# First attention mixer: scores in two PSUM banks by turns, turned rows in one bank instead of two

## The chip, the cores and the metric

The kernel runs on one core of one Trainium2 chip. The metric is the device time of one launch in microseconds (us), the median of several runs; lower is better. TensorE is PE in the profile, VectorE DVE, ScalarE ACT, GpSimd POOL and SyncE SP.

## What is computed

A trunk of two layers over 512 tokens of width 1024. Each layer is half a SwiGLU block, an attention mixer and another half SwiGLU block; each sub-layer has an RMS norm, a shift and scale made from a condition vector, and a gated residual add. The first layer's mixer ("mixA", layer "A" in the code) is the one that is changed. Cut to what matters:

```python
def moba_mixer(h, w_qkv, w_o, cos, sin):
    qkv = (h @ w_qkv).reshape(B, S, 3, N_HEADS, HEAD_DIM)
    q, k = apply_rope(qkv[:, :, 0], cos, sin), apply_rope(qkv[:, :, 1], cos, sin)
    return moba_attention(q, k, qkv[:, :, 2]).reshape(B, S, ATTN_DIM) @ w_o
# moba_attention: 2 blocks of 256 tokens, top 3 of the past blocks: with 512 tokens
# every past block is chosen, so it is causal softmax attention, 16 heads of 64
p = softmax(where(causal, q @ k.T * scale, -inf)); o = p @ v
```

## The kernel before, in words

All matrix products run in float32 split into a high and a low part, three passes each (L412, L413, L414: high by high, low by high, high by low). Weights come by DMA in units of 512 KB into w_raw (L397); ScalarE copies the high part into w_hi (L403), VectorE, sometimes GpSimd, subtracts to get w_lo (L407).

**The mixer's work in steps.** mixA handles 16 heads in four groups of four. A head has four steps, one for each 128 query tokens, so there are 64 steps, numbered here 0 to 63; step n has n % 4 + 1 tiles of 128 keys. The steps of one group run beside the q, k and v projections of the next group ("substeps" on TensorE), and the last group's beside the output projection. The order of work on each engine is written out by hand as program code; engines meet through counting semaphores. For step n the chain is:

- TensorE: *score n*, two matmuls (L805, L806) into a PSUM bank.
- VectorE: *negmax n*, which scales and masks the scores, writes them to SBUF and keeps the row maximum (L2157, with its read-accumulator row behind it).
- ScalarE: exp n (L1965); VectorE: reciprocal of the sum, n (L2177); GpSimd: scaling by it (L2358).
- TensorE: *turn n*, n % 4 + 1 transposes of the probabilities into a PSUM bank (L839). The bank holds the "turned rows".
- ScalarE: *copy n*, the high part of the turned rows (L1989); VectorE: *subtraction n*, the low part (L2221). Both read the bank of the turned rows. After four steps TensorE multiplies by v (L849), and ScalarE and VectorE fold the result (L1998, L2233).

**Where they stand.** The programs are skewed. TensorE's `begin(n)` does score n, one or two substeps of the projection (L412 to L414) where the table has any for that step, and then turn n-2. VectorE's `begin(n)` does negmax n, reciprocal n-1, the fold of a head where one is due, and then subtraction n-3; behind it stand, by hand-written tables, other work of the step: a w_lo subtraction (L407), half of a rotary multiply (L1528), the low part of rotated rows (L1577). ScalarE's `begin(n)` does exp n, then what its tables say (w_hi, L403; high part of rotated rows, L1572; v, L1607), and at the end copy n-2.

**The banks.** PSUM has eight banks. In mixA the projections take 0 to 3, the scores have bank 4, the heads' output 5, and the turned rows take 6 and 7 by turns. So score n waits until negmax n-1 has read bank 4, and turn n waits until subtraction n-2 has read its bank. The second mixer, layer "B", has scores in 4 and 3 and turned rows in 6 and 7; it keeps both.

Of the kernel before, what the change touches and what calls it, by code (L numbers as in the profile page):

```python
# [32 lines left out]
P = 128  # L33
# [146 lines left out]
def build(nc, x_t, c_col, ada_first, ada, ada_bias, gains, gate_up, down, mixa_w, kv_w, mixb_w, cos_t, sin_t,  # L180
          mask_a, mask_b, lanes_in, ident_in, out):
    with ExitStack() as ctx:  # L182
# [3 lines left out]
        def sb(stack, name, shape, dt=F32):  # L186
            return stack.enter_context(nc.sbuf_tensor(name, shape, dt))
# [10 lines left out]
        ident = sb(ctx, "ident", [P, P])  # L198
# [31 lines left out]
        with ExitStack() as mixer_space:  # L230
# [10 lines left out]
            pt_hi = sb(mixer_space, "pt_hi", [P, 4, 4, P], F32R)  # L241
# [17 lines left out]
        ps = ctx.enter_context(nc.psum_tensor("ps", [P, 8, 512], F32))  # L259
# [12 lines left out]


        def scores(layer, st):
            return ps[:, 4 if layer == "A" or st % 2 == 0 else 3, :]

        def turned(st):
            return ps[:, 6 + st % 2, :].rearrange("p (n q) -> p n q", n=4)

        o_ps = ps[:, 5, :]  # L280

# [4 lines left out]
        def second_pt(tile):  # L286
            return flat(tile)[:, 2 * S:6 * S].rearrange("p (n i q) -> p n i q", n=4, i=4)

        pt_a = ((pt_hi[:], pt_lo[:]), (second_pt(q_st), second_pt(k_hi)))
        spare_slots = v_out[:].rearrange("p j t a d -> p (j t a d)")[:, 0:2 * S].rearrange("p (n s) -> p n s", n=2)  # L290

        def p_slot(layer, st):
            n = st % SLOTS[layer]
            return probs[:, n, :] if n < 6 else spare_slots[:, n - 6, :].bitcast(F32)
# [47 lines left out]
        def per_mixer(name):  # L342
            return {"A": sem(name + "_a"), "B": sem(name + "_b")}

        s_done, negmax_done, exp_done = per_mixer("s_done"), per_mixer("negmax_done"), per_mixer("exp_done")
        factor_done, scaled_done = per_mixer("factor_done"), per_mixer("scaled_done")
        t_done, pt_hi_done, pt_lo_done = per_mixer("t_done"), per_mixer("pt_hi_done"), per_mixer("pt_lo_done")
# [396 lines left out]
        def pe_mixer(pe, name):  # L744
            layer = name[-1]
            is_a = layer == "A"
# [46 lines left out]
            def score(st):  # L793
                h, i, sl = st // 4, st % 4, st // 4 % 2
                if i == 0:
                    pe.wait_ge(k_landed[h % 2], 32 * ((hd0 + h) // 2 + 1))
                    pe.wait_ge(q_landed[h % 2], 16 * ((hd0 + h) // 2 + 1))
                    if h % 4 == 0 and not is_a:
                        pe.wait_ge(q_direct, h // 4 * 16 + 32)
                tile, s_ps = slice(i * P, (i + 1) * P), scores(layer, st)  # L800
                if is_a:
                    if st >= 1:
                        pe.wait_ge(negmax_done["A"], st)
                    past = slice(0, (i + 1) * P)
                    nc.tensor.matmul(s_ps[:, past], q_st[:, 0, sl, tile], k_hi[:, 0, sl, past], start=True, stop=False)  # L805
                    nc.tensor.matmul(s_ps[:, past], q_st[:, 0, sl, tile], k_lo[:, 0, sl, past],  # L806
                                     start=False, stop=True).then_inc(s_done["A"], 1)
                    return


                if st >= 2:
                    pe.wait_ge(negmax_done["B"], 2 * st - 2)
                if st >= 6 and i == 2:
                    pe.wait_ge(exchanged, 2 * h - 1)
                q, past = q_st[:, sl, 0, tile], slice(max(i - 1, 0) * P, (i + 1) * P)
                kh, kl = k_hi[:, sl, 0, past], k_lo[:, sl, 0, past]
                o = s_ps[:, P if i == 0 else 0:2 * P]
                nc.tensor.matmul(o, q, kh, start=True, stop=False)
                nc.tensor.matmul(o, q, kl, start=False, stop=True)
                for b in (1, 2):  # L820
                    o, q = s_ps[:, (1 + b) * P:(2 + b) * P], q_st[:, sl, b, tile]
                    nc.tensor.matmul(o, q, k_hi[:, sl, b, tile], start=True, stop=False)
                    mm = nc.tensor.matmul(o, q, k_lo[:, sl, b, tile], start=False, stop=True)
                mm.then_inc(s_done["B"], 1)
# [7 lines left out]

            def transpose_p(st):
                pe.wait_ge(scaled_done[layer], st + 1)
                if st >= 2:
                    pe.wait_ge(pt_lo_done[layer], st - 1)
                i = st % 4
                for n in range(i + 1) if is_a else range(1 if i == 0 else 0, 4):
                    mm = nc.tensor.transpose(turned(st)[:, n, :], p_slot(layer, st)[:, n * P:(n + 1) * P], ident[:])  # L839
                mm.then_inc(t_done[layer], 1)  # L840

            def weigh_a(h):
# [44 lines left out]
            def begin(st, first=(), second=()):  # L887
                if st < ROWS:
                    score(st)
                for part in first:  # L890
                    part()
                back = st - lag
                if is_a and back >= 5 and back % 4 == 1:
                    weigh_a(back // 4 - 1)
                if not is_a and back >= 4 and back % 4 < 2:
                    weigh_b(back // 4 - 1, back % 4)
                for part in second:
                    part()
                if 0 <= back < ROWS:
                    transpose_p(back)  # L900
                if not is_a and st % 4 == 0 and 4 <= st <= ROWS:
                    exchange(st // 4 - 1)
# [1036 lines left out]
        def act_mixer(act, name):  # L1939
            layer = name[-1]  # L1940
            is_a, lag = layer == "A", LAG[layer]
# [36 lines left out]
            def round_pt(st):  # L1978
                i = st % 4
                act.wait_ge(t_done[layer], st + 1)  # L1980
                if is_a:
                    h = st // 4
                    if h >= 2 and i == 0:
                        act.wait_ge(pv_done["A"], h - 1)
                    src, dst = turned(st)[:, 0:i + 1, :], pt_a[h % 2][0][:, 0:i + 1, i, :]
                else:
                    first = 1 if i == 0 else 0
                    src, dst = turned(st)[:, first:4, :], pt_hi[:, i, first:4, :]
                nc.scalar.copy(dst, src).then_inc(pt_hi_done[layer], 1)  # L1989

            def fold_copy(h):
# [14 lines left out]
            def collect(st):  # L2006
                if (st - lag) % 4 == 1 and st - lag >= 5:
                    fold_copy((st - lag) // 4 - 1)
                if 0 <= st - lag < ROWS:
                    round_pt(st - lag)  # L2010
# [137 lines left out]
        def dve_mixer(dve, name, g_block, col_n, stored):  # L2148
            layer = name[-1]
            is_a, lag = layer == "A", LAG[layer]  # L2150
# [4 lines left out]
            def masked(st, cols, mask, lowest):  # L2155
                dve.sem_inc(carrier, 1)
                nc.vector.tensor_tensor_reduce(  # L2157
                    out=p_slot(layer, st)[:, cols], in0=scores(layer, st)[:, cols], in1=mask, scale=-(HD ** -0.5),
                    scalar=FAR, op0=ALU.add, op1=ALU.min, accum_out=lowest).then_inc(negmax_done[layer], 1)
# [54 lines left out]
            def split_pt(st):  # L2214
                i = st % 4
                dve.wait_ge(pt_hi_done[layer], st + 1)
                first = 1 if i == 0 and not is_a else 0
                src = turned(st)[:, 0:i + 1, :] if is_a else turned(st)[:, first:4, :]
                hi, lo = (pt[:, 0:i + 1, i, :] if is_a else pt[:, i, first:4, :]
                          for pt in (pt_a[st // 4 % 2] if is_a else (pt_hi, pt_lo)))  # L2220
                nc.vector.tensor_tensor(lo, src, hi.bitcast(F32), ALU.subtract).then_inc(pt_lo_done[layer], 1)  # L2221
# [29 lines left out]
            def collect(st):  # L2251
                if (st - lag) % 4 == 1 and st - lag >= 5:
                    fold_add((st - lag) // 4 - 1)
                if 0 <= st - lag < ROWS:
                    split_pt(st - lag)
# [458 lines left out]
```

## Time and profile before

| what | value |
|---|---|
| median of 3 runs | 2371.2 us (2370.36 to 2376.19) |
| profiled execution: its time, its span from first to last instruction | 2373.33 us, 2371.5 us |
| granted TensorE clock, mean | 0.994 of full |
| TensorE busy / VectorE / ScalarE / GpSimd, share of span | 99% / 55% / 37% / 12% |
| attention steps of mixA in the trace | 457 to 646 us |

The profile comes from one execution with a hardware profiler. Its busy time of TensorE counts overlapping matmuls: a matmul of 512 columns is shown 0.39 us long while the next starts 0.23 us after it. So a short stop of TensorE can lie inside "busy", and the start times of successive rows say more than the busy share.

### The profile page before, as it was taken

How to read it: one execution, taken by the hardware profiler on the slowest of the kernel's cores; microseconds unless marked ns; L12 is line 12 of the kernel's file. 1: busy time of each engine (PE TensorE's matmuls, PEld its weight loads, DVE VectorE, ACT ScalarE, POOL GpSimd, SP SyncE). 2: the span in 40 equal slices, each digit the busy share in tenths (PEclk: the TensorE clock that was granted, in tenths of full speed). 3: DMA queues.
4: the chain of work that ended last, by engine and by line, in shares of the span. 5: the costliest groups of instructions: out<-in, count | busy, mean ns of one | idle time of the engine just before them, and what ended most of it. 6: DMA issues, size and time to landing. Idle time of an engine off the chain costs nothing. (4 is left out here: it accounts for less than half of the span.)

```text
span 2371.5 us, 31348 instructions
## 1 busy us (share of the span) xinstructions
PE 2337.0 (99%) x11240; PEld 1941.8 (82%) x11245; DVE 1315.5 (55%) x2084; ACT 876.4 (37%) x1397; POOL 288.8 (12%) x373
## 2 busy tenths in 40 slices
PE   9999999999999999999999999999999999999998
PEld 6888888788878888888888888888888887888886
DVE  7555544776675554465554555544777766333333
ACT  3322223456543332233332333322456654333221
POOL 0000000244300000003232000000134531000000
PEclk9999999999999999999999999999999989999999
DMA  6666543577456564338777666543788862333332
GB/s 249 198 188 192 177 133 100 200 245 247 159 157 197 184 187 131 115 97 273 238 236 252 233 196 189 159 144 96 229 294 295 297 237 73 97 97 97 93 97 85
DMA packets 128896, 424.90 MB, mean 179 GB/s; under 512 B 14112, under 2 KB 22944, under 8 KB 128288
## 3 DMA queue, kind: packets, MB, share of 16 engines
q1 hardware_dynamic: 111392, 356.55, 46.9%
q0 software_dynamic: 17408, 67.12, 8.1%
q8 instruction: 54, 0.88, 0.2%
q14 instruction: 42, 0.34, 0.0%
HBM read 352.84 MB, written 69.21 MB: 178 GB/s over the span
## 5 line engine op out<-in xcount | busy, mean ns | idle before, releaser
L407 DVE TENSOR_TENSOR w_lo<-w_raw,w_hi 128x1024 fp32r<-128x1024 f32 (+2 forms) x382 | 467.8, 1225 | 610.2 <-ACT w_hi L403 609.8
L412 PE MATMUL ps<-h_hi,w_hi 128*128 128x512 f32 x1872 | 741.7, 396 | 9.2 <-POOL h_lo L2101 2.5
L414 PE MATMUL ps<-h_hi,w_lo 128*128 128x512 f32 x1872 | 730.9, 390 | 0.0
L413 PE MATMUL ps<-h_lo,w_hi 128*128 128x512 f32 x1872 | 730.6, 390 | 0.0
L403 ACT CAST w_hi<-w_raw 128x1024 fp32r<-128x1024 f32 (+2 forms) x388 | 395.6, 1020 | 752.5 <-PE ps L414 735.6
L412 PEld LDWEIGHTS ps<-h_hi,w_hi 128*128 128x128 f32 x1872 | 352.8, 188 | 84.6 <-issue 6.1
L414 PEld LDWEIGHTS ps<-h_hi,w_lo 128*128 128x128 f32 x1872 | 352.4, 188 | 74.9
L413 PEld LDWEIGHTS ps<-h_lo,w_hi 128*128 128x128 f32 x1872 | 353.0, 189 | 68.7 <-issue 0.2
L412 PE MATMUL ps<-act_hi,w_hi 128*128 128x512 f32 x704 | 275.3, 391 | 0.0
L414 PE MATMUL ps<-act_hi,w_lo 128*128 128x512 f32 x704 | 274.1, 389 | 0.0
L413 PE MATMUL ps<-act_lo,w_hi 128*128 128x512 f32 x704 | 273.9, 389 | 0.0
L1553 POOL TENSOR_TENSOR rotated<-tmp 128x512 f32<-128x512 f32 x32 | 44.5, 1391 | 1309.7 <-DVE tmp L1107 1229.7
L1420 DVE TENSOR_TENSOR prod<-ps,silu_g 128x512 f32<-128x512 f32 x86 | 59.5, 692 | 260.1 <-ACT silu_g L1376 260.1
L976 DVE SCALAR_TENSOR_TENSOR ada_acc<-ada_raw,c_act,ada_acc 128x1024 f32<-128x1024 f32 x126 | 161.2, 1280 | 0.7
L412 PEld LDWEIGHTS ps<-act_hi,w_hi 128*128 128x128 f32 x704 | 132.1, 188 | 31.0 <-issue 3.9
L414 PEld LDWEIGHTS ps<-act_hi,w_lo 128*128 128x128 f32 x704 | 132.2, 188 | 27.6
L413 PEld LDWEIGHTS ps<-act_lo,w_hi 128*128 128x128 f32 x704 | 132.2, 188 | 27.2
L1376 ACT ACTIVATE silu_g<-ps 128x512 f32<-128x512 f32 x86 | 51.5, 599 | 252.1 <-PE ps L414 251.7
L1376 ACT ACT_TABLE_LOAD x30 | 38.5, 1283 | 135.0 <-PE ps L414 135.0
L412 PE MATMUL ps<-w_hi,kv_h_hi 128*128 128x512 f32 x192 | 74.8, 390 | 0.0
L413 PE MATMUL ps<-w_lo,kv_h_hi 128*128 128x512 f32 x192 | 74.7, 389 | 0.0
L414 PE MATMUL ps<-w_hi,kv_h_lo 128*128 128x512 f32 x192 | 74.7, 389 | 0.0
(206 smaller groups left out, 2798.3 us busy)
## 6 DMA issues: line engine op xcount, KB each, us to landing
w_raw<-gate_up SPq DMA_DIRECT2D x176, 512.0 KB, 3.7
ada_raw<-ada SPq DMA_DIRECT2D x144, 512.0 KB, 4.6
w_raw<-down SPq DMA_DIRECT2D x80, 512.0 KB, 3.6
w_raw<-kv_w SPq DMA_DIRECT2D x48, 512.0 KB, 3.8
w_raw<-mixa_w SPq DMA_DIRECT2D x34, 512.0 KB, 4.2
w_raw<-mixb_w SPq DMA_DIRECT2D x34, 512.0 KB, 4.9
kb<-rot_st POOLq DMA_DIRECT2D x24, 512.0 KB, 4.9
kb<-att POOLq DMA_DIRECT2D x24, 512.0 KB, 5.2
```

Of the source, the lines that this page charges most:

```text
L403: nc.scalar.copy(w_hi[:, slot, 0:n], w_raw[:, slot, 0:n]).then_inc(w_hi_done, 1)
L407: eng.tensor_tensor(w_lo[:, slot, 0:n], w_raw[:, slot, 0:n], w_hi[:, slot, 0:n].bitcast(F32), ALU.subtract).then_inc(w_lo_done[slot], 2)
L412: nc.tensor.matmul(out_ap, l_hi, r_hi, start=start, stop=False, skip_group_check=skip)
L413: nc.tensor.matmul(out_ap, l_hi, r_lo, start=False, stop=False, skip_group_check=skip)
L414: return nc.tensor.matmul(out_ap, l_lo, r_hi, start=False, stop=stop, skip_group_check=skip)
L976: nc.vector.scalar_tensor_tensor(out=ada_acc[:], in0=ada_raw[:, slot, :], scalar=c_act[:, k:k + 1], in1=ada_acc[:], op0=ALU.mult, op1=ALU. ...
L1376: nc.scalar.activation(silu_g[:, b, :], ps[:, 2 * b, :], ACT.Silu).then_inc(silu_done, 1)
L1420: nc.vector.tensor_tensor(prod[:, b, :], ps[:, 2 * b + 1, :], silu_g[:, b, :], ALU.mult).then_inc(pair_free, 1)
L1553: nc.gpsimd.tensor_tensor(*operands(0), ALU.subtract).then_inc(rope_done, 1)
```

## The change

In layer "A" the scores get bank 4 on even steps and bank 6 on odd ones, and all turned rows go to bank 7. Score n then waits for negmax n-2 instead of n-1, and turn n for subtraction n-1 instead of n-2. Nothing else differs: no instruction is added, removed or moved on any engine, and layer "B" is as it was.

```diff
         def scores(layer, st):
-            return ps[:, 4 if layer == "A" or st % 2 == 0 else 3, :]
-
-        def turned(st):
-            return ps[:, 6 + st % 2, :].rearrange("p (n q) -> p n q", n=4)
+            return ps[:, 4 if st % 2 == 0 else 6 if layer == "A" else 3, :]
+
+        def turned(layer, st):
+            return ps[:, 7 if layer == "A" else 6 + st % 2, :].rearrange("p (n q) -> p n q", n=4)
...
                 if is_a:
-                    if st >= 1:
-                        pe.wait_ge(negmax_done["A"], st)
+                    if st >= 2:
+                        pe.wait_ge(negmax_done["A"], st - 1)
...
             def transpose_p(st):
                 pe.wait_ge(scaled_done[layer], st + 1)
-                if st >= 2:
-                    pe.wait_ge(pt_lo_done[layer], st - 1)
+                if st >= (1 if is_a else 2):
+                    pe.wait_ge(pt_lo_done[layer], st if is_a else st - 1)
```

(The other lines of the diff pass the layer to `turned` where ScalarE and VectorE read the bank.)

TensorE's program at the start of the attention steps, score 1: k_hi, k_lo and q_st are the operands of a score.

```order
 L413 MATMUL ps<-h_lo,w_hi 128x512
 L414 MATMUL ps<-h_hi,w_lo 128x512
-L805 MATMUL ps<-k_hi,q_st 128x256 [waits negmax_done_a]
+L805 MATMUL ps<-k_hi,q_st 128x256
 L806 MATMUL ps<-k_lo,q_st 128x256
 L412 MATMUL ps<-h_hi,w_hi 128x512
```

Score 1 no longer waits; the scores after it keep a wait, for a count that is one lower.

TensorE's program two steps on (its begin(3)), turn 1: probs are the probabilities, and pt_lo_done_a counts the subtractions.

```order
 L413 MATMUL ps<-h_lo,w_hi 128x512
 L414 MATMUL ps<-h_hi,w_lo 128x512
-L839 MATMUL ps<-ident,probs 128x128 [waits scaled_done_a]
+L839 MATMUL ps<-ident,probs 128x128 [waits pt_lo_done_a,scaled_done_a]
 L839 MATMUL ps<-ident,probs 128x128
 L805 MATMUL ps<-k_hi,q_st 128x128 [waits negmax_done_a,q_landed1,k_landed1]
```

Turn 1 now waits for subtraction 0; the turns after it waited for a subtraction before and now wait for the next one. No row has moved on TensorE, and the other engines' programs are the same row for row.

## Rows read from the trace of the kernel before

**Rows 1.** Waits of TensorE, 450 to 660 us: total, times, longest

```profile
PE ps L805 <- DVE negmax L2157: 3.2, 4, 1.2
PE ps L839 <- DVE pt_lo L2221: 1.0, 1, 1.0
PE ps L805 <- issue: 0.9, 1, 0.9
PE ps L412 <- DVE x L2117: 0.9, 1, 0.9
PE ps L412 <- POOL h_lo L2101: 0.5, 1, 0.5
```

**Rows 2.** Timeline of TensorE: start, length, row, idle before; score 1, turn 28, score 31

```profile
460.27 0.39 PE L805 MATMUL ps<-k_hi,q_st 128*128 128x256 f32 x1 [1.19 <-DVE negmax L2157]
...
541.71 0.27 PE L839 MATMUL ps<-ident,probs 128*128 128x128 f32 x1
542.67 0.50 PE L805 MATMUL ps<-k_hi,q_st 128*128 128x512 f32 x1 [0.69 <-DVE negmax L2157]
```

**Rows 3.** Timeline, SyncE's load of q for score 4, and score 4

```profile
463.43 0.43 SPq L1755 DMA_DIRECT2D q_st<-qa  x1
...
469.67 0.30 PE L805 MATMUL ps<-k_hi,q_st 128*128 128x128 f32 x1 [0.86 <-issue]
```

**Rows 4.** Timeline of TensorE, second group of heads: turns 18, 24 and 26

```profile
520.25 0.49 PE L839 MATMUL ps<-ident,probs 128*128 128x128 f32 x3
...
533.77 0.27 PE L839 MATMUL ps<-ident,probs 128*128 128x128 f32 x1
...
538.91 0.49 PE L839 MATMUL ps<-ident,probs 128*128 128x128 f32 x3
```

**Rows 5.** Timeline of VectorE, second group: subtractions 17, 23, 25 and 27

```profile
520.27 0.43 DVE L2221 TENSOR_TENSOR pt_lo<-ps,pt_hi 128x256 fp32r<-128x256 f32 x1
...
534.32 0.69 DVE L2221 TENSOR_TENSOR k_hi<-ps,q_st 128x512 fp32r<-128x512 f32 x1 [1.00 <-ACT q_st L1989]
...
539.19 0.42 DVE L2221 TENSOR_TENSOR pt_lo<-ps,pt_hi 128x256 fp32r<-128x256 f32 x1
...
542.73 0.69 DVE L2221 TENSOR_TENSOR pt_lo<-ps,pt_hi 128x512 fp32r<-128x512 f32 x1
```

**Rows 6.** Timeline of ScalarE: work ahead of copies 23 and 27, and the copies

```profile
532.76 1.05 ACT L1572 CAST rot_st<-rotated 128x1024 fp32r<-128x1024 f32 x1
533.71 0.58 ACT L1989 CAST q_st<-ps 128x512 fp32r<-128x512 f32 x1
...
541.17 1.05 ACT L403 CAST w_hi<-w_raw 128x1024 fp32r<-128x1024 f32 x1 [0.28 <-PE ps L414]
542.12 0.58 ACT L1989 CAST pt_hi<-ps 128x512 fp32r<-128x512 f32 x1
```

**Rows 7.** Timeline, third group: turn 44 (TensorE) and subtraction 43 (VectorE)

```profile
590.82 0.30 PE L839 MATMUL ps<-ident,probs 128*128 128x128 f32 x1
...
592.54 0.69 DVE L2221 TENSOR_TENSOR pt_lo<-ps,pt_hi 128x512 fp32r<-128x512 f32 x1 [0.74 <-ACT pt_hi L1989]
```

**Rows 8.** Timeline, last group: turns 50 and 51, subtractions 49 and 50

```profile
609.91 0.55 PE L839 MATMUL ps<-ident,probs 128*128 128x128 f32 x3
...
611.30 0.42 DVE L2221 TENSOR_TENSOR pt_lo<-ps,pt_hi 128x256 fp32r<-128x256 f32 x1
...
611.88 0.63 PE L839 MATMUL ps<-ident,probs 128*128 128x128 f32 x4 [0.99 <-DVE pt_lo L2221]
...
612.84 0.56 DVE L2221 TENSOR_TENSOR pt_lo<-ps,pt_hi 128x384 fp32r<-128x384 f32 x1 [0.70 <-ACT pt_hi L1989]
```

**Rows 9.** Busy time by windows (us; engines; PEclk; DMA share, GB/s): mixA, and mixB's end

```profile
457.00:646.00 189.00, 182.47 (x1085) 159.61 (x1084) 126.59 (x338) 111.15 (x251) 79.69 (x104) 1.00 0.67 230
...
1895.00:1905.00 10.00, 6.43 (x42) 5.80 (x42) 7.05 (x25) 5.13 (x16) 3.76 (x8) 0.93 0.92 332
1905.00:1915.00 10.00, 10.00 (x47) 9.56 (x47) 4.42 (x15) 4.29 (x14) 2.78 (x5) 0.56 0.92 325
```

More of the change, by code:

```diff
@@ L834, in transpose_p @@
                 pe.wait_ge(scaled_done[layer], st + 1)
-                if st >= 2:
-                    pe.wait_ge(pt_lo_done[layer], st - 1)
+                if st >= (1 if is_a else 2):
+                    pe.wait_ge(pt_lo_done[layer], st if is_a else st - 1)
                 i = st % 4
                 for n in range(i + 1) if is_a else range(1 if i == 0 else 0, 4):
-                    mm = nc.tensor.transpose(turned(st)[:, n, :], p_slot(layer, st)[:, n * P:(n + 1) * P], ident[:])
+                    mm = nc.tensor.transpose(turned(layer, st)[:, n, :], p_slot(layer, st)[:, n * P:(n + 1) * P], ident[:])
                 mm.then_inc(t_done[layer], 1)
@@ L1984, in round_pt @@
                         act.wait_ge(pv_done["A"], h - 1)
-                    src, dst = turned(st)[:, 0:i + 1, :], pt_a[h % 2][0][:, 0:i + 1, i, :]
+                    src, dst = turned(layer, st)[:, 0:i + 1, :], pt_a[h % 2][0][:, 0:i + 1, i, :]
                 else:
                     first = 1 if i == 0 else 0
-                    src, dst = turned(st)[:, first:4, :], pt_hi[:, i, first:4, :]
+                    src, dst = turned(layer, st)[:, first:4, :], pt_hi[:, i, first:4, :]
                 nc.scalar.copy(dst, src).then_inc(pt_hi_done[layer], 1)
@@ L2217, in split_pt @@
                 first = 1 if i == 0 and not is_a else 0
-                src = turned(st)[:, 0:i + 1, :] if is_a else turned(st)[:, first:4, :]
+                src = turned(layer, st)[:, 0:i + 1, :] if is_a else turned(layer, st)[:, first:4, :]
                 hi, lo = (pt[:, 0:i + 1, i, :] if is_a else pt[:, i, first:4, :]
```

## The prediction

> **What bounds the kernel now.** TensorE is busy for 99% of the span. In mixA I read the waits of TensorE first. Five kinds are all there are, 6.5 us together: scores that wait for negmax (3.2 us, four times), a turn that waits for a subtraction (1.0 us), one "issue" wait (0.9 us) and two waits of the output projection (0.9 and 0.5 us) [rows 1]. All else that TensorE does there it does back to back, so a delay that is put on it is made up nowhere unless it falls into one of these waits. The reader should see next that the old score wait costs little and where: score 1 stands idle for 1.19 us, and score 31 starts 0.96 us after turn 28 although only one small transpose lies between [rows 2]. Scores 15 and 47 are the same place in the other groups; these are the steps that have no projection work between two scores.
>
> Then I read, for each step n, where turn n starts and where subtraction n-1 ends. The change makes the first wait for the second. Before the change this distance is free, so it may be negative, and in 34 of 63 steps it is negative or too short. That is what the prediction rests on.
>
> **The wait that is removed.** Scores 15, 31 and 47 each come up by 0.96 us less the 0.06 us that a 128-column transpose takes (a quarter of the 0.23 us from one 512-column matmul to the next): 0.9 us, 2.7 us for three. Score 1 comes up by 1.19 us idle and 0.16 us that the row of the matmul before it hides (0.39 us shown, next start after 0.23 us): 1.35 us. But score 4 follows in the same stretch and waits 0.86 us for "issue", which is the landing of its q and k: the q load left at 463.43 and the score began at 469.67 [rows 3]. The load hangs on weights' split and on stores, not on score 1, so an earlier score 1 only makes score 4 wait longer. I take 0 for score 1; if the load does come earlier, it is a gain of 1.35 us.
>
> **The wait that is added.** Queued behind a waiting turn n on TensorE are score n+3, the next projection matmuls and so everything. What a waiting TensorE needs after the end of the instruction that it waits for is seen twice: turn 51 began at 611.88, 0.16 us after subtraction 49 ended (611.30 + 0.42) [rows 8]. With 0 and 0.16 us as its bounds I take 0.10 us; 0.05 us more or less is 1 us over some twenty waits. The shortfall of turn n is then end of subtraction n-1, plus 0.10, less start of turn n.
>
> Second group, steps 16 to 31 [rows 4, 5]:
> - turn 18: 520.27 + 0.43 + 0.10 - 520.25 = 0.55 us.
> - turn 24: 534.32 + 0.69 + 0.10 - 533.77 = 1.34 us.
> - turn 26: 539.19 + 0.42 + 0.10 - 538.91 = 0.80 us.
> - turn 28: 542.73 + 0.69 + 0.10 - 541.71 [rows 2] = 1.81 us.
> - turns 20 and 22 come out between the first and the third of these in the same two views, 0.39 and 0.86 us.
>
> Turns 18 to 26 are four small ones and turn 24 one large, with turn 28 six in all, 5.75 us. Two more, turns 21 and 25, are short by under 0.4 us but drop out: VectorE was then working off a queue and does not shift with TensorE's new delay. For the same reason I take 0.4 off turn 22 and 0.3 off turn 26. That leaves 5.05 us.
>
> Why don't the later ones vanish once TensorE has waited? Because the two large ones have a cause that moves with TensorE. Copy 23 runs at 533.71 behind rotated rows' high part (532.76, 1.05 us), and copy 27 at 542.12 behind w_hi, which started at 541.17 when TensorE released it (0.28 us idle, ended by PE) [rows 6]. A TensorE that is later releases them later. VectorE's subtraction follows the copy at once (534.32 with 1.00 us of idle ended by ACT, [rows 5]).
>
> Groups: the second gives 5.05 - 0.9 = **+4.1 us**. The first repeats it without turn 18 (no fold is due there yet): 4.5 - 0.9 = **+3.6 us**. The third also has the output's inputs on ScalarE, which puts copies back: turn 44 is short by 592.54 + 0.69 + 0.10 - 590.82 = 2.51 us [rows 7] in place of 1.81; turn 40 by 1.0 instead of 1.3; turns 34, 36, 38 and 42 by 0.55, 0.39, 0.47 and 0.4. Turn 46 too is short, by 0.9 us, but the matmul right behind its score waited 0.9 us for VectorE's addition to x anyway [rows 1], so this costs nothing. Sum 5.3 - 0.9 = **+4.4 us**.
>
> Last group: three steps stand without projection work there. Turn 50 is short by 611.30 + 0.42 + 0.10 - 609.91 = 1.91 us. Turn 51 by 612.84 + 0.56 + 0.10 - 611.88 = 1.62 us, but it already waited 0.99 us, and both its old wait and subtraction 50 move with turn 50, so only 0.1 us is new. Turns 48, 49 are short by 0.5 us together, turns 52 to 60 by about 1.6 us. The 0.5 us wait for h_lo behind it [rows 1] and a little of VectorE's queue are filled by the delay, 0.75 us off. **+3.4 us**.
>
> Sum: 3.6 + 4.1 + 4.4 + 3.4 = **15.5 us**. After mixA nothing gives it back: what follows is a serial norm and TensorE-bound GEMM. The profiled execution took 2373.33 us, span 2371.5; it would become 2388.8. It stood 2.1 us above the median of the runs, 2371.2, so I give 2371.2 + 15.5 = **2386.7 us**.
>
> **A page against the trace.** The bank that is given up matters because in each step both ScalarE and VectorE read what TensorE wrote, one after the other: copy 23 from 533.71 to 534.29, subtraction 23 from 534.32 to 535.01 [rows 5, 6], so with one bank the next turn can't overlap either. The Trainium skill, "PSUM — Partial Sum Buffer", section "PSUM bank collisions raise a hardware error", says that TensorE, ScalarE and VectorE may not touch the same bank and partitions at once, and asks for semaphores by bank; by that rule the new wait can be neither dropped nor narrowed to columns, and the score's second bank is paid for in full. A sum by the old score wait alone would be -4.1 us; by the new one it is +15.5. The trace agrees as far as it goes: copy and subtraction of a step never overlap in these rows.
>
> **The rivals.**
> - *Each wait resets the lag.* While TensorE waits, VectorE and ScalarE catch up, and the shortfalls behind it in the group vanish; only the largest of each group is left: 1.34 or 1.81, less 0.9, in two groups, 2.5 - 0.9 in the third, 1.9 in the last. 0.9 + 0.9 + 1.6 + 1.9 = 5.3 us, 2376.5 us, within 0.3%. For it: VectorE has 35% of idle in mixA (126.59 of 189 us busy [rows 9]). Against: turns 24 and 28 hang on work that TensorE itself releases. Chance 0.12.
> - *The other side: the turns were never late.* The subtraction has room before the turn if VectorE and ScalarE, now given score 1, 15, 31, 47 earlier, pull ahead for the rest of the group. Place: turns 20 to 28; price: all shortfalls gone, gain 2.7 + 1.35 = 4.1 us, 2367.1 us. It decides for a gain if less than 4.1 us of the 18.2 us of shortfalls that I counted (15.5 + 2.7) survives. Against it: the earlier scores number four, and each comes at a group's end, behind the turns in question. Chance 0.04.
> - *No absorption.* All 34 shortfalls, read as above but with 0.07 us in place of 0.10, come to 26.1 us (5.5, 6.0, 8.8 and 5.9 by group), less 2.7: +23.4, 2394.6 us. Chance 0.08.
> - *The clock falls.* In all of mixA the granted clock is 1.00, that is 2.4 GHz, with TensorE busy 182.47 of 189 us. At mixB's end TensorE was busy 6.43 of 10 us, and in the next 10 us the clock was 0.56, so nearly all of it at 1.2 GHz [rows 9]: 0.44 x 10 = 4.4 us of work lost. The last group of mixA now gets 3.5 us of waits within 6 us (turns 50 and 51). 15.5 + 4.4 = 19.9, 2391.1 us. Chance 0.10. The Trainium skill, "TensorE: Matmul & The Clock Gate", part 1, says that the throttled clock is the default and only activity lifts it; by that rule such a gap of waits may cost a stretch at half rate, and the trace at mixB's end agrees.
>
> The forecast itself keeps 0.66.
>
> **How the numbers follow.** 0.3% is 7.1 us, about what a measurement of this kernel can tell from no change. The forecast's own range: lower end, only the turns whose cause moves with TensorE and turn 50, 3.15 - 0.9 twice, 3.5 - 0.9, 1.9, less 1.35 for score 1: 7.7 us, 2378.9; upper end the 23.4 us above, 2394.6. The range reaches down into the first rival and to the upper bound: 2376 to 2394.5. Slower than by 0.3%: 0.66, 0.08 and 0.10, 0.84. Within 0.3%: the first two rivals, 0.12 and 0.04, less 0.02 for a gain above 7.1 us, which none of the cases reaches and which I keep as what I have not seen: 0.14 and 0.02.
>
> **What the changed profile would show.** Waits of TensorE in mixA: the negmax rows at L805 gone or nearly, and L839 waiting for pt_lo (L2221) some 20 times for 12 to 19 us in place of 1.0. Score 4 begins at about the same time as before. Turns 24 and 28 are late by more than a microsecond each against the row before them, and the four groups lengthen by 3 to 5 us each. ScalarE, VectorE and GpSimd keep their busy time; the second mixer keeps its length. I am wrong if L839's waits are few, or if they are many but other waits disappear by as much, or if work outside mixA changes.

## The result: 19 us slower

The changed kernel takes 2391.9 us (median of 4 runs, 2391.0 to 2392.8) against 2372.6 us of the kernel before in the same comparison: a ratio of 1.0081, 95% interval [1.0069, 1.0093]. A second measurement gave 1.0083 [1.0069, 1.0096]. The forecast was 2386.7 us, range 2376 to 2394.5, slower with a chance of 0.84.

The waits of TensorE in the profile after, 450 to 690 us, answer to [rows 1]. Columns: who waited for whom, us in total, times, longest.

```profile
PE ps L839 <- DVE pt_lo L2221: 11.9, 15, 2.2
PE ps L839 <- DVE k_hi L2221: 5.2, 10, 1.2
PE ps L805 <- issue: 2.4, 1, 2.4
...
```

The scores' waits for negmax are gone, and the turns wait 25 times for a subtraction (both tiles are written by L2221), 17.1 us in place of 1.0. The two waits of the output projection (for x and h_lo) are gone too. The "issue" wait is score 4's and has grown from 0.9 to 2.4 us, while score 4 begins 12.5 us after score 0 as against 12.3 us before. (What else the window holds are two waits of TensorE behind mixA, which the kernel before has too.)

The same turns as in [rows 2, 4], and score 31, in the timeline of TensorE after:

```profile
527.71 0.52 PE L839 MATMUL ps<-ident,probs 128*128 128x128 f32 x3 [0.43 <-DVE pt_lo L2221]
...
543.54 0.30 PE L839 MATMUL ps<-ident,probs 128*128 128x128 f32 x1 [1.19 <-DVE k_hi L2221]
...
553.93 0.30 PE L839 MATMUL ps<-ident,probs 128*128 128x128 f32 x1 [1.66 <-DVE pt_lo L2221]
553.98 0.48 PE L805 MATMUL ps<-k_hi,q_st 128*128 128x512 f32 x1
```

Turns 18, 24 and 28 wait, and turn 26 too (0.41 us, at 549.25). Score 31 follows turn 28 after 0.05 us instead of 0.96 us. VectorE after, subtractions 23 and 27 and the negmax ahead of the second, as in [rows 5]:

```profile
542.70 0.69 DVE L2221 TENSOR_TENSOR k_hi<-ps,q_st 128x512 fp32r<-128x512 f32 x1 [0.95 <-ACT q_st L1989]
...
552.44 0.56 DVE L2157 CUSTOM_DVE_ANT_0 probs<-ps,m_a 128x384 f32<-128x384 f32 x1 [1.30 <-issue]
553.09 0.69 DVE L2221 TENSOR_TENSOR pt_lo<-ps,pt_hi 128x512 fp32r<-128x512 f32 x1
```

Turn 24 starts 0.15 us after subtraction 23 ends (542.70 + 0.69), turn 28 0.15 us after subtraction 27 ends (553.09 + 0.69).

**Where the time went.** Groups are taken from score 0, 16, 32 and 48 to the next of these, the last to the last transpose of turn 63 (us, from the timelines):

| | first | second | third | last | mixA |
|---|---|---|---|---|---|
| before | 46.7 | 48.9 | 47.8 | 42.2 | 185.5 |
| after | 52.3 | 53.3 | 53.7 | 47.2 | 206.5 |
| longer by | 5.6 | 4.4 | 6.0 | 5.0 | 21.0 |

A part of it is the clock. The windows of the profile after show half speed, 1.2 GHz, in three places in mixA (the value after the busy times is PEclk), where [rows 9] have 1.00 for all of mixA:

```profile
471.50:475.00 3.50, 3.50 (x13) 2.80 (x12) 0.70 (x4) 1.69 (x4) 0.69 (x1) 0.51 0.86 331
608.00:611.50 3.50, 3.50 (x10) 2.72 (x9) 2.76 (x7) 2.00 (x5) 2.36 (x3) 0.51 0.19 27
632.00:635.50 3.50, 3.50 (x13) 2.81 (x12) 1.23 (x4) 1.30 (x3) 0.54 (x2) 0.52 0.76 303
```

Each costs half of 3.4 us, 1.7 us. What TensorE did just before the first two stands in its timeline: a long wait each time, and within 1 us after it matmuls that are shown 0.63 us long instead of 0.39. Before the third it waited 1.88 us for turn 50 and 1.28 us for turn 51. That the wait brings the low clock is so far only what the order of the rows suggests; runs 4 to 6 test it.

```profile
471.12 0.30 PE L805 MATMUL ps<-k_hi,q_st 128*128 128x128 f32 x1 [2.44 <-issue]
...
607.40 0.30 PE L839 MATMUL ps<-ident,probs 128*128 128x128 f32 x1 [2.23 <-DVE pt_lo L2221]
...
608.36 0.63 PE L413 MATMUL ps<-h_lo,w_hi 128*128 128x512 f32 x1
```

Without them the groups are longer by 3.9, 4.4, 4.3 and 3.3 us, 15.9 us together. Outside mixA the changed kernel's profiled execution is 1.5 us shorter than that of before: in mixB (the second mixer) half clock lasted 17.0 us before and 10.2 us after, at the program's start 6.8 us before and 10.2 us after.

For all runs there is a rough split: span times (1 - mean granted clock) is what half clock cost, within 1.2 us per run since the clock is given to 0.001. Over 41 runs of before it is 12.8 us and over 9 of the changed kernel 16.7 us; the rest of the span is 2357.7 and 2372.9 us. So of 19.1 us (the difference of the mean spans), about **15.2 us are waits and 3.9 us clock**.

### The profile page after: what moved, and what is told of

It reads as the page before. It is cut to its first block and busy times, and to the rows that moved or that the text cites. A ratio compares the mean times of both kernels' runs of the same rounds, so it can differ in the third digit from the quotient of the medians.

```text
span 2391.0 us, 31354 instructions
## 1 busy us (share of the span) xinstructions
PE 2344.5 (98%) x11245; PEld 1942.7 (81%) x11245; DVE 1315.0 (55%) x2084; ACT 878.0 (37%) x1397; POOL 289.6 (12%) x373
## 5 line engine op out<-in xcount | busy, mean ns | idle before, releaser
L839 PE MATMUL ps<-ident,probs 128*128 128x128 f32 x336 | 57.9, 282 | 17.3 <-DVE pt_lo L2221 11.9
```

What stands on the lines that cost most here:

```text
L839: mm = nc.tensor.transpose(turned(layer, st)[:, n, :], p_slot(layer, st)[:, n * P:(n + 1) * P], ident[:])
```

## The experiments

Each ratio is against runs of the kernel before on the same chip. "At full clock" is the rest of the span as just defined, against that of those same runs of before. Since the clock is given to 0.001, differences of a microsecond in it are not to be relied on.

**1. Turned rows alone.** The new sharing of bank 7, without the scores' second bank:

```diff
-            return ps[:, 4 if st % 2 == 0 else 6 if layer == "A" else 3, :]
+            return ps[:, 4 if layer == "A" or st % 2 == 0 else 3, :]
...
-                    if st >= 2:
-                        pe.wait_ge(negmax_done["A"], st - 1)
+                    if st >= 1:
+                        pe.wait_ge(negmax_done["A"], st)
```

> One half of the change alone: turned rows share bank 7 as in the changed kernel, scores have bank 4 only as before. Theory W (the new wait of the turns costs all of it, the second score bank gives back 2.7 us): slower than the changed kernel by 2.7 us at scores 15, 31 and 47; score 1 waits again, score 4 then waits under 1 us instead of 2.4 us, and the stretch of low clock that followed it in the changed kernel (1.7 us) may go. Against the kernel before +19 to +23 us. Rival R (the second score bank itself costs, by earlier scores that collide with VectorE's queue): faster than the changed kernel, under +15 us against before.

2389.5 us, ratio 1.0073 [1.0061, 1.0085]; +14.8 us at full clock, where the changed kernel has +15.2. The expected 2.7 us on top are not there. The median is 18.3 us above before: under theory W's +19 to +23, and over rival R's +15. Two points of theory W did come: score 1 waits 1.19 us and score 4 not at all, and there is no low clock behind score 4; the clock's cost is 14.7 us per run in place of 16.7. Groups two to four take 53.3, 52.1 and 47.3 us; the second is the changed kernel's to 0.02 us. TensorE around turn 28 and score 31, and VectorE there:

```profile
551.33 0.30 PE L839 MATMUL ps<-ident,probs 128*128 128x128 f32 x1 [1.66 <-DVE pt_lo L2221]
551.39 0.48 PE L805 MATMUL ps<-k_hi,q_st 128*128 128x512 f32 x1
```

```profile
549.85 0.56 DVE L2157 CUSTOM_DVE_ANT_0 probs<-ps,m_a 128x384 f32<-128x384 f32 x1 [1.30 <-issue]
...
550.49 0.69 DVE L2221 TENSOR_TENSOR pt_lo<-ps,pt_hi 128x512 fp32r<-128x512 f32 x1
```

Score 31 must wait for negmax 30 here, and doesn't stand still for it. Turn 28, ahead of it, waits for subtraction 27, and that stands behind negmax 30 on VectorE. Once the turned rows have one bank, the new wait contains the old one. It holds from score 4 on: turn n-3 stands ahead of score n and waits for subtraction n-4, which VectorE does behind negmax n-1. Scores 2 and 3 do not stand still in this run. So except for score 1 the second score bank has nothing left to give: scores 15, 31 and 47 come up by 0.90 us each here as in the changed kernel. Theory W falls in this point; so does rival R.

**2. Scores alone.** Turned rows keep two banks; some scores use bank 5, which the heads' output leaves free in steps with n % 4 = 1 and 2:

```diff
         def scores(layer, st):
-            return ps[:, 4 if layer == "A" or st % 2 == 0 else 3, :]
+            if layer == "A":
+                return ps[:, 5 if st == 1 or st % 4 == 2 and st != 2 else 4, :]
+            return ps[:, 4 if st % 2 == 0 else 3, :]
...
-                    if st >= 1:
-                        pe.wait_ge(negmax_done["A"], st)
+                    if st % 4 == 2 and st != 2:
+                        pe.wait_ge(att_done["A"], st // 4 - 1)
+                    elif st > 1:
+                        pe.wait_ge(negmax_done["A"], st - 1 if st == 2 or st % 4 == 3 and st != 3 else st)
```

(The product with v, which writes bank 5, waits for the last negmax that reads it.)

> The other half alone, by another way to a bank: turned rows keep banks 6 and 7; score 1 and every third score of a head (n % 4 = 2) go to bank 5, which the heads' output does not use then, all others to bank 4, so scores 15, 31 and 47 need not wait for the negmax just before them. Theory W: faster than before by 2.7 us (three times 0.9 us), 0 from score 1 since score 4 waits for its q either way, 0.9 us turning into some 2.2 us of wait; if that wait brings a stretch of low clock, 1.7 us of it is lost again: -1 to -3 us. Rival R (the score side costs by itself): 0 to +5 us.

2371.8 us, ratio 0.9995 [0.9985, 1.0004], which is not clear of no change; -2.0 us at full clock. Score 15 and score 31 each gave 0.93 us. Score 1's gain was lost as forecast: the wait of score 4 in this kernel's list is

```profile
PE ps L809 <- issue: 2.6, 1, 2.6
```

No stretch of half clock follows this wait, the longest of score 4's in any run; behind it PEclk is 1.00:

```profile
469.50:473.00 3.50, 3.48 (x19) 2.99 (x20) 1.60 (x9) 2.24 (x6) 1.00 (x2) 1.00 0.85 267
```

Of score 47's 0.9 us, 0.6 us were gone before score 48, and 0.7 us more went at turn 54, where the output projection now waits for w_lo (two waits, 1.0 us in the list); why w_lo is late there was not looked into.

**3. Scores alone, without score 1.** The same, but score 1 stays in bank 4 and waits:

```diff
-                return ps[:, 5 if st == 1 or st % 4 == 2 and st != 2 else 4, :]
+                return ps[:, 5 if st % 4 == 2 and st > 2 else 4, :]
...
-                    elif st > 1:
-                        pe.wait_ge(negmax_done["A"], st - 1 if st == 2 or st % 4 == 3 and st != 3 else st)
+                    elif st >= 1:
+                        pe.wait_ge(negmax_done["A"], st - 1 if st % 4 == 3 and st != 3 else st)
```

> Turned rows keep banks 6 and 7; scores with n % 4 = 2 from step 6 on go to bank 5, and score 1 keeps its wait (in the run that also gave score 1 a bank, its 1.3 us only lengthened the wait of score 4). Theory W: scores 15 and 31 come up by 0.9 us each, score 47 by 0.9 us of which some 0.6 us are lost at once, so mixA is 1.5 to 2.5 us shorter at full clock, and the wait of score 4 stays under 1 us: median 0 to 2.5 us under the kernel before. Rival: no difference in mixA.

2368.9 us, ratio **0.9986 [0.9977, 0.9995]**, the one kernel here whose interval lies below 1, if barely: 2.6 us less at full clock. In its profile mixA is only 0.9 us shorter (184.6 us; again about 1 us is lost at turn 54), so of the 2.6 us only 0.9 us are found in the trace; the rest may be the spread between runs. It is well ahead of the changed kernel, and ahead of the kernel before by little.

**4. Matmuls in the waits.** The changed kernel with idle matmuls, into a score bank that is free, at four waits (10 ahead of score 4, 9 ahead of turn 44, 7 and 4 ahead of turns 50 and 51):

```diff
+                if is_a and st == 4:
+                    pe.wait_ge(negmax_done["A"], 3)
+                    pe_keep_busy(10, 4)
...
             def transpose_p(st):
+                if is_a and st in (44, 50, 51):
+                    pe.wait_ge(negmax_done["A"], st + 2)
+                    pe_keep_busy({44: 9, 50: 7, 51: 4}[st], 4 if st % 2 else 6)
```

> The changed kernel with matmuls on idle data put into four of its waits (10 ahead of score 4, 9 ahead of turn 44, 7 and 4 ahead of turns 50 and 51; each 0.22 us, all shorter together than the wait they stand in). Results are unchanged. Theory C (5.1 us of the 19.3 us are three stretches of half clock in mixA that follow long waits): the three stretches are gone from mixA, 3 to 5 us faster than the changed kernel. Rival (the low clock in the profile is chance or costs nothing, the waits are all): same as the changed kernel within 1 us, or slower by what the extra matmuls add.

The profile has the expected effect: mixA takes 201.6 us in place of 206.5, with the full clock all through (PEclk 1.00):

```profile
457.00:659.00 202.00, 189.06 (x1101) 158.75 (x1100) 125.43 (x336) 112.31 (x250) 81.79 (x104) 1.00 0.61 212
```

But the median of its runs is 2391.6 us, ratio 1.0086 [1.0073, 1.0099]: no better than the changed kernel. The clock's cost falls from 16.7 to 13.9 us per run, and the rest rises from 2372.9 to 2375.0 us. Only one run of five, the profiled one at 2385.6 us, is as fast as its profile would have it. So the theory fails as a way to gain. That the matmuls took the low clock away is not shown by this profile alone either: run 5 has full clock behind an unfilled turn 44, and run 6 behind unfilled turns 50 and 51.

**5. The same at score 4 alone** (nine matmuls).

```diff
+                if is_a and st == 4:
+                    pe.wait_ge(negmax_done["A"], 3)
+                    pe_keep_busy(9, 4)
```

> The changed kernel with nine matmuls on idle data (2 us together) in the wait of score 4 alone, which is 2.4 us in the changed kernel. Results are unchanged. Theory C (the 3.4 us of half clock behind score 4 come from that wait): no low clock between 465 and 480 us, group 1 shorter by 1.7 us, group 1 otherwise the same; median 0 to 2 us under the changed kernel, since the other stretches of low clock vary from run to run. Rival: the low clock stays there, or group 1 keeps its 52.3 us.

2388.9 us, ratio 1.0070 [1.0057, 1.0084]; +16.3 us at full clock, and 13.9 us of clock per run in place of 16.7. The median is 3.0 us under the changed kernel's, somewhat more than the 0 to 2 us expected. The first group takes 50.2 us in place of 52.3, the other groups 53.4, 52.2 and 47.2. The window of 465 to 480 us has PEclk 1.00, where the changed kernel has 0.89:

```profile
465.00:480.00 15.00, 14.68 (x91) 11.91 (x91) 10.90 (x30) 8.79 (x21) 6.59 (x12) 1.00 0.74 275
```

The low clock behind score 4 is gone with the wait filled. But the third group is 1.6 us shorter as well (52.2 in place of 53.7 us), and there nothing was filled. Turn 44 waits as long as in the changed kernel, and no half clock follows:

```profile
603.89 0.30 PE L842 MATMUL ps<-ident,probs 128*128 128x128 f32 x1 [2.24 <-DVE pt_lo L2224]
```

```profile
603.00:607.50 4.50, 3.61 (x20) 3.20 (x21) 3.35 (x8) 3.48 (x9) 3.35 (x4) 1.00 0.14 28
```

**6. The changed kernel again.** No edit.

> The changed kernel a second time, to see which of its stretches of low clock come back. If they belong to the waits: one behind score 4 (about 470 us) again and one or two near turns 44 and 50 (600 to 640 us), mixA 205 to 208 us; at full clock 15 to 17 us more than before. If they are chance: at other places in mixA, or none.

2391.6 us, ratio 1.0083. The low clock came back at 471.6 us and at 608.1 us, not at 632: two of the three places, and mixA takes 204.7 us. Score 4 waited only 1.7 us this time.

All profiles together (the wait that was left standing, in us, and whether 3.4 us or more of half clock began in it or within 1.4 us behind it):

| place | half clock | none |
|---|---|---|
| score 4 | changed kernel 2.4, run 6 1.7, runs 7 and 8 2.3, run 9 2.0 | run 2 2.6 |
| turn 44 | changed kernel and run 6 2.2, run 8 2.7 | runs 1 and 5 2.2, run 7 1.6, run 9 1.1 |
| turns 50, 51 | changed kernel, runs 1, 5 and 7 1.9 and 1.3, runs 8 and 9 2.5 and 1.9 | run 6 1.9 and 1.3 |
| turn 12 | run 8 1.9 | all others, 1.1 to 1.7 |
| turn 28 | | run 8 1.9, all others 1.1 to 1.7 |

Where the waits were filled (score 4 in runs 4 and 5, the turns in run 4) no half clock followed. So in the steps of mixA half clock came only at long waits, but not at each: waits of 2.2 us at turn 44 had it in two profiles and lacked it in two others. That a wait is needed is well supported. What else decides is not shown, and no single place is sure.

**7. Copy first.** In the changed kernel ScalarE does copy n-2 right after exp n in the steps where it otherwise did w_hi, rotated rows, v or output inputs first:

```diff
                     begin(a * STEPS + s)
+                    copy_first = is_a and (s in (9, 13) or not early and s in (10, 11, 12, 14))
+                    if copy_first:
+                        collect(a * STEPS + s)
...
-                    collect(a * STEPS + s)
+                    if not copy_first:
+                        collect(a * STEPS + s)
```

> The changed kernel with ScalarE's copy of the turned rows put ahead of its w_hi, rotated rows, v and output-input work in steps 9 and 13 of each group (in the third also 10, 11, 12 and 14). Theory A (the large shortfalls, turns 8, 12, 24, 28, 40, 44, come from the copy standing behind 1 us operations): each falls by about 1 us, 6 to 9 us faster than the changed kernel in all, with clock stretches less up to 10. Rival (VectorE's own queue holds the subtraction back, ScalarE's order does not matter): under 2 us.

2388.9 us, ratio 1.0071 [1.0058, 1.0084]; +11.6 us at full clock, 3.6 us less than the changed kernel, between theory and rival. The waits around turns 8, 24 and 40 fell by 1.1, 1.1 and 0.6 us (24 from 1.37 to 0.32 us, read against turn 23), and that of turn 44 by 0.7 us. Turns 12 and 28 hardly changed. Around turn 28, in order of time:

```profile
547.73 0.63 PE L839 MATMUL ps<-ident,probs 128*128 128x128 f32 x4
...
548.39 0.59 ACT L1989 CAST pt_hi<-ps 128x512 fp32r<-128x512 f32 x1 [0.70 <-PE ps L839]
...
549.44 0.67 DVE L2225 TENSOR_TENSOR pt_lo<-ps,pt_hi 128x512 fp32r<-128x512 f32 x1
...
550.26 0.30 PE L839 MATMUL ps<-ident,probs 128*128 128x128 f32 x1 [1.55 <-DVE pt_lo L2225]
```

Copy 27 now follows turn 27 at once, and turn 28 still waits 1.55 us (1.66 before this edit). Four transposes, a copy and a subtraction of 512 columns are 0.63 + 0.59 + 0.67 = 1.9 us by themselves, and in the kernel before turn 28 starts only 0.8 us after turn 27 does (540.92 and 541.71), because step 30 has no projection. With one bank, that part of the wait remains in any order. Another part is VectorE's order: subtraction 27 starts 0.46 us after copy 27 has ended (548.39 + 0.59), behind negmax 30. In run 9, with subtraction 27 first, turn 28 waits 1.14 us.

**8. Subtraction first.** VectorE does subtraction n-3 ahead of negmax n:

```diff
+                if is_a:
+                    collect(st - 1)
                 if st < ROWS:
                     negated_max(st)
...
-                collect(st - 1)
+                if not is_a:
+                    collect(st - 1)
```

> The changed kernel with VectorE's subtraction n-3 (and the fold where due) put ahead of negmax n instead of behind it. Theory V (in the smaller shortfalls, turns 18, 22, 26, 50 and 58, the subtraction is late because it stands behind negmax n on VectorE, not because its copy is late): turn 18 no longer waits, turns 22 and 26 wait 0.4 to 0.5 us less each, turns 24 and 28, which are held by the copy, wait as long as before; 3 to 5 us faster than the changed kernel. Rival (negmax, exp and scaling come later in exchange and make the turns wait for the scaling): same as the changed kernel or slower.

2396.2 us, ratio 1.0097 [1.0081, 1.0112]: slower than the changed kernel, +19.6 us at full clock. Turn 18 no longer waits and turn 26's wait falls from 0.6 to 0.2 us, as theory V has it. But negmax, exp and with them the copies come later, and turns 20 and 22 lose 0.9 and 1.0 us where they lost 0.3 and 0.4. Turns 24 and 28, which were to stay as they were, lose 1.6 and 2.1 us instead of 1.3 and 1.8. A subtraction that waits for its copy now holds up the next negmax. The theory was right on the cause at turns 18 and 26 and wrong on the sum. The rival has the sum right, but not the wait: no turn waits for the scaling in this profile, they all wait for subtractions.

**9. Both orders.** Edits 7 and 8 together.

> The changed kernel with both orders: copy first on ScalarE (as in the run that put the copy first, which took about 4 us off mixA apart from the clock) and subtraction ahead of negmax on VectorE. If the two causes are separate: 7 to 9 us less than the changed kernel in mixA at full clock, so 7 to 9 us more than before are left. Rival (one shortfall only uncovers the other): as the better of the two alone, 4 to 5 us less than the changed kernel.

2389.4 us, ratio 1.0073 [1.0059, 1.0086]; +11.9 us at full clock, as copy first alone. The rival is right in the sum: turn 28 gains (1.14 us of wait in place of 1.55), while turns 20 and 22 lose as in run 8.

## Why the prediction was right, and where it was not

- **The number.** Forecast were 15.5 us on top of 2371.2, measured were 19.3 us on top of 2372.6. The waits make 15.2 of them, and the clock 3.9, for which the sum had no term.
- **The distance from subtraction n-1 to turn n** is the quantity that decided. It forecast the waits where they came (turns 18, 20, 22, 24, 26, 28 and their like), and the groups at full clock: 3.6, 4.1, 4.4 and 3.4 us forecast, 3.9, 4.4, 4.3 and 3.3 us measured; 15.5 against 15.9 in the profile and 15.2 over the runs. Turn by turn in the second group the forecast was 0.55, 0.39, 0.46, 1.34, 0.50 and 1.81 us, and the delays that each turn adds in the profile are 0.59, 0.33, 0.43, 1.33, 0.56 and 1.82 us; turn 44 adds 2.39 us where 2.51 were forecast. So the sum is not right by errors that cancel. The expected 12 to 19 us of waits at L839 are 17.1 us. That each group lengthens by 3 to 5 us holds at full clock; with the clock the first and third are 5.6 and 6.0 us longer.
- **The latency** was taken as 0.10 us and is 0.15 us at each such wait in the profile after; over 25 waits that is 1.2 us, within what the corrections for VectorE's queue were worth. The prediction says that it was seen twice, but cites one place, and that one has 0.16 us.
- **The removed wait.** The 2.7 us came (0.90 us at each of scores 15, 31 and 47), but the scores' second bank did not bring them. In the changed kernel they follow from the added wait (run 1). The net was right since I subtracted a gain that exists either way; the forecast for that experiment, which rested on the reason, was wrong.
- **Score 1 and score 4.** That the 1.35 us would only lengthen score 4's wait was right (2.4 us, run 2: 2.6 us). That half clock may follow such a wait I did not cost.
- **The clock** was put as a rival with 4.4 us and a chance of 0.10, at turns 50 and 51. The forecast's own sum had nothing for it, and this is the term that was mis-sized: it adds 3.9 us over the runs. The place was right: half clock began at turns 50 and 51 in six of the seven profiles that left their waits standing. But score 4 and turn 44, which the rival does not name, had it too in some. 15.5 + 4.4, that rival's 2391.1 us, is within 1 us of what was measured; that 4.4 us at one place comes so near to 3.9 us from several is luck. The Trainium skill, "TensorE: Matmul & The Clock Gate", part 1, has two clock levels and activity that lifts the lower one. The rows of 0.51, each behind a wait, agree with that; the long waits without half clock (2.6 us in run 2) show that a wait alone does not foretell it.
- **The first rival** gave VectorE 35% of idle time in mixA; 126.59 of 189 us busy is 33%. Nothing hangs on it: the later shortfalls of a group did not vanish.
- **Cause of the large shortfalls.** "Copy 23 behind rotated rows" is right for turn 24 (run 7). "Copy 27 behind w_hi" is not the cause at turn 28: the chain of turn, copy and subtraction is longer than TensorE's way from turn 27 to turn 28, whatever stands in front of the copy, and negmax 30 ahead of the subtraction adds 0.4 us (runs 7 and 9).

Open: why the output projection waits for w_lo at turn 54 in runs 2 and 3, why run 4's other executions do not show the gain of its profile, and what decides whether half clock follows a long wait.

## What to carry to other kernels

Before two buffers are made one, measure for each user the distance between the last reader of the previous content and the next writer; where it is negative, the missing time is the price, and a step with no filler work between two writers pays the whole chain of write, copy and subtract. Before a buffer is added, ask whether a wait that stays already implies the one it removes: two waits on one in-order engine cost only the later. A wait of some 2 us on TensorE can cost more than its length: here half clock followed in some profiles and not in others, at 1.7 us each time it lasted 3.4 us. Before a stretch of low clock is put down to one wait, look for the same wait in other profiles.

## What the runs showed of the hardware that was not expected

- Single waits of TensorE, in a stretch where it otherwise works without a stop, were followed by 3.4 us at half clock, 1.7 us of loss each: 2.4 us (in the other profile of the changed kernel 1.7 us) at score 4 and 2.2 us at turn 44 in both profiles of the changed kernel. The same length is no guarantee: 2.2 us at turn 44 in runs 1 and 5 and 2.6 us at score 4 in run 2 were not followed by it, nor was turn 28's wait of 1.66 us in either profile of the changed kernel.
- The spread between runs of the kernel before (2368.6 to 2378.3 us in 41 runs on three chips) goes with the mean granted clock: 0.996 in its three fastest runs and 0.993 in its six slowest. At full clock the same runs spread about half as much (a standard deviation of 1.2 us in place of 2.2).
